# First feed-forward of a two-block model: gate borders as a ScalarE bias, gelu in PSUM, value taps moved, loops rotated

## The chip, the cores and the metric

One core of a Trainium2 chip runs the whole program. The metric is the device time of one execution in microseconds. In the text PE is TensorE (matmul), DVE is VectorE, ACT is ScalarE, POOL is GpSimd and SP is SyncE, which only issues loads here. SBUF is the working memory; PSUM is the memory that PE writes, eight banks of 128 x 512 f32.

## The reference

Two transformer-like blocks run one after the other on x of 1024 positions by 1024 channels, in f32. The change touches only the feed-forward of the first:

```python
h = _rmsnorm(x, ffn_pre_norm[l])
u = _causal_depthwise_conv(h @ w_up[l], conv_w[l], conv_b[l])    # CONV_WIDTH = 3
gate, val = jnp.split(u, 2, axis=-1)                             # D_FF = 2816 each
y = (jax.nn.gelu(gate, approximate=True) * val) @ w_down[l]
```

The convolution runs over the positions: each output is the bias plus three taps, of the same position and of the two before it. The feed-forward of the second block has no convolution.

## The kernel before

**Tiling.** Channels and features lie on the 128 partitions, positions along the free axis, in two halves LO and HI of HALF = 512. A "feature" n is a strip of 128 gate features and the 128 value features beside it; there are 22. Weights and activations are split into a high and a low part, and each product is three matmuls (high x high, high x low, low x high). Features 4 to 19 of each feed-forward are done in eight *pairs* with a fast scheme of seven block products where eight would be usual: one for the up product of each feature and one for the down product of the pair.

**PE.** `pair_up` (L1428) does seven `pair_block`s (L1415) of twelve matmuls for one feature; they go to bank 0 (gate, lower half), 1 (gate, upper half), 3 (value, upper half) and 2 (value, lower half), and DVE's sums complete them. `pair_down` (L1458) does seven blocks of four products into banks 4 to 7, each block into all four again. The order is: first feature of a pair, down product of the pair before, second feature. Each block waits for its bank to be read out (semaphores `lin_first`, `g_cv`, `p_prod`, `c_sum`, `p_lo`, `dn_free`) and for its weights (`unit_split`).

**DVE (L3338 to L3411).** `pair_unit1` is the work on one feature: `first_sums`, two gate taps of the lower half (`gate_taps`, L3348), `second_value` (completes bank 3), in a first feature `last_lows` of the pair before, `second_gate` (completes bank 1), a gate tap of the upper half, `first_value` (the last sum, completes bank 2), the other gate tap, and `edge_taps` (L3356): the two columns at the border of the halves need the last columns of bank 0, which ACT copied to EDGE because PE has filled bank 0 again by then. `gated_value` then does the value taps (L3367) and the product with gelu (L3373) for the upper half, and the same for the lower half, into banks 3 and 2. `first_blocks` and `second_blocks` form from these products the sums and the low parts for the down product (L3201, L3205). `pair_sums` (L3249) adds the 28 results of a down product to Y1t in SBUF. `pair_step1` strings these together and is the body of a loop.

**ACT (L2297 to L2405).** `gate_first` and `gate_second` write bias + third tap of the gate into ST_GATE in SBUF (L2302, L2309) and keep the border columns (L2304). `value_lin` (L2319) does the same for the value into ST_VALUE, `gelu_half` (L2314) works in place in ST_GATE. `product_high` and `sum_high` write high parts (L2188, L2192), `cast` writes high parts of weights (L2184). Its loop body is two times `pair_step1`: `first_up1`, `down_casts1`, `second_up1`. So it starts with `value_lin` and `gelu_half` of the second feature of the pair before.

**POOL** forms the weights' sums and low parts (L932, L939, L941, L944), and **SP** issues the weight loads.

Each engine runs its instructions in the order written out here; nothing is scheduled at run time. Behind the eighth pair comes a tail: two more features in halves (`half_tile` on PE, `unit_taps`, `product1` and `unit_low` on DVE), with the last pair's down product between them. In the tail DVE does the units' work first and then all of `pair_sums`.

## Time and profile before

| | us |
|---|---|
| median of 3 runs | 2838.39 (2836.68 to 2843.15) |
| the profiled execution | 2840.2, of which the span is 2838.4 |
| PE busy | 2702.7 (95%) |
| DVE busy | 1777.6 (63%) |
| POOL busy | 1700.1 (60%) |
| ACT busy | 971.9 (34%) |
| mean granted clock of PE | 0.987 |

The span is what the profile shows; the execution's time holds 1.8 us more around it. The features 4 to 19 of the first feed-forward lie at about 775 to 1333 us of the span, those of the second at about 2300 to 2778. In a timeline row the first two numbers are start and duration in us; "x28" says that a row merges 28 instructions; the bracket at the end is the time in which the engine did nothing before the row, and what ended it.

### The profile page before, as it was taken

Reading aid. Unit: us, or ns where it says so; the run is one execution under the profiler, and the core shown is the slowest. Engines: PE = TensorE matmul, PEld = TensorE weight load, DVE = VectorE, ACT = ScalarE, POOL = GpSimd, SP = SyncE. Lnnn points to the kernel's source line nnn. Section 1 sums busy time; section 2 is a strip of 40 time slices with the busy share of each in tenths; the row PEclk is TensorE's granted clock in tenths of the full one; section 3 lists DMA queues with packets and bytes.
Section 4 is the critical chain, followed back from the end, with each engine's and each line's share of the span. In section 5 each row is a group of like instructions: output and inputs, shape, how many; then the busy total and the mean of one; then the engine's idle time right before and its main releaser. Section 6 shows DMA issues by size and latency. Waiting matters only on the chain.

```text
span 2838.4 us, 39050 instructions
## 1 busy us (share of the span) xinstructions
PE 2702.7 (95%) x12922; PEld 2148.6 (76%) x12922; DVE 1777.6 (63%) x2540; ACT 971.9 (34%) x1941; POOL 1700.1 (60%) x1264
## 2 busy tenths in 40 slices
PE   8999999898989999998899999998999999999998
PEld 5777777686867777776678888777877878888887
DVE  6666687748568888877744311475536256766667
ACT  5544444435222233322423112555234222222222
POOL 4566311356988878875433334221355998888974
PEclk9999999999999999999999999999999999999999
DMA  4322221044111111114241234221444111111134
GB/s 143 101 89 88 92 90 49 12 147 161 38 52 53 53 49 52 52 50 157 90 144 49 59 107 141 88 73 53 141 148 165 51 49 56 57 55 55 53 123 141
DMA packets 89222, 243.01 MB, mean 86 GB/s; under 512 B 8527, under 2 KB 12400, under 8 KB 88692
## 3 DMA queue, kind: packets, MB, share of 16 engines
q1 hardware_dynamic: 66992, 183.27, 20.5%
q10 hardware_dynamic: 22084, 57.86, 5.8%
q8 instruction: 84, 1.38, 0.2%
q14 instruction: 62, 0.51, 0.1%
HBM read 205.95 MB, written 32.52 MB: 84 GB/s over the span
## 4 chain that ended last, share of the span: by engine, by line
PE 78%; DVE 11%; issue 4%; ACT 3%; POOL 3%; DMA 1%; DVEq 0%; POOLq 0%; ACTq 0%; SPq 0%
PE ps L1049 13%; PE ps L1051 12%; PE ps L1050 12%; PE ps L1422 6%; PE ps L1424 6%; PE ps L1423 6%; PE ps L1469 3%; PE ps L1471 3%; PE ps L1470 3%; PE ps L1140 2%; PE ps L1156 2%; PE ps L1704 1%; PE ps L1716 1%; PE ps L1171 1%; DVE ps L2954 1%
## 5 line engine op out<-in xcount | busy, mean ns | idle before, releaser
L797 POOL CAST wh<-raw 128x1024 fp32r<-128x1024 f32 x171 | 184.7, 1080 | 826.4 <-PE ps L1051 770.6
L1049 PE MATMUL ps<-hh,wh 128*128 128x512 f32 x1456 | 599.6, 412 | 24.9 <-DVE hl L2914 11.0
L1051 PE MATMUL ps<-hh,wl 128*128 128x512 f32 x1456 | 572.2, 393 | 0.0
L1050 PE MATMUL ps<-hl,wh 128*128 128x512 f32 x1456 | 570.7, 392 | 0.0
L799 POOL TENSOR_TENSOR wl<-raw,wh 128x1024 fp32r<-128x1024 f32 x171 | 412.5, 2412 | 13.7
L1049 PEld LDWEIGHTS ps<-hh,wh 128*128 128x128 f32 x1456 | 275.7, 189 | 97.6 <-issue 16.2
L1051 PEld LDWEIGHTS ps<-hh,wl 128*128 128x128 f32 x1456 | 274.8, 189 | 60.2
L1050 PEld LDWEIGHTS ps<-hl,wh 128*128 128x128 f32 x1456 | 275.8, 189 | 52.1 <-issue 3.4
L932 POOL TENSOR_TENSOR wl<-raw,wh 128x512 fp32r<-128x512 f32 x138 | 192.1, 1404 | 101.3 <-ACT wh L2184 100.8
L827 POOL TENSOR_TENSOR arena<-arena 128x1023 f32<-128x1023 f32 (+7 forms) x64 | 115.0, 1809 | 103.2 <-ACT arena L2041 100.8
L1423 PE MATMUL ps<-al,wh 128*128 128x512 f32 x420 | 165.6, 394 | 0.0
L3249 DVE TENSOR_TENSOR hlf<-ps,hlf 128x512 f32<-128x512 f32 x224 | 152.4, 691 | 20.9 <-PE ps L1471 19.0
L2184 ACT ACTIVATE wh<-raw 128x512 fp32r<-128x512 f32 x138 | 85.0, 627 | 203.6 <-PE ps L1471 134.2
L3249 DVE TENSOR_TENSOR arena<-ps,arena 128x512 f32<-128x512 f32 x224 | 146.8, 687 | 3.5 <-PE ps L1471 1.7
L3097 DVE TENSOR_TENSOR_SCAN arena<-arena,reset 128x1024 f32<-128x1024 f32 (+7 forms) x64 | 104.6, 1673 | 65.8 <-ACT arena L2038 65.8
L1049 PE MATMUL ps<-ah,wh 128*128 128x512 f32 x320 | 128.3, 401 | 5.8 <-DVE al L2986 3.1
L941 POOL TENSOR_TENSOR wl<-weight_sum,wh 128x512 fp32r<-128x512 f32 x92 | 124.4, 1353 | 7.4
L1051 PE MATMUL ps<-ah,wl 128*128 128x512 f32 x320 | 125.3, 392 | 0.0
L1050 PE MATMUL ps<-al,wh 128*128 128x512 f32 x320 | 125.1, 391 | 0.0
L2047 ACT ACTIVATE arena<-ps 128x512 f32<-128x512 f32 (+3 forms) x144 | 70.8, 492 | 158.6 <-PE ps L1156 158.0
L3183 DVE TENSOR_TENSOR ps<-ps,arena 128x512 f32<-128x512 f32 x96 | 66.9, 696 | 80.5 <-PE ps L1424 71.3
L1422 PE MATMUL ps<-hh,wh 128*128 128x512 f32 x240 | 96.4, 402 | 19.1 <-DVE block L3205 19.1
(412 smaller groups left out, 6334.3 us busy)
## 6 DMA issues: line engine op xcount, KB each, us to landing
raw<-weights SPq DMA_DIRECT2D x181, 512.0 KB, 3.6
raw<-weights SPq DMA_DIRECT2D x176, 256.0 KB, 2.6
arena<-w_ada SPq DMA_DIRECT2D x48, 512.0 KB, 3.8
arena<-gate_scratch ACTq DMA_DIRECT2D x20, 512.0 KB, 4.8
arena<-x_t ACTq DMA_DIRECT2D x1, 4096.0 KB, 14.0
x_scratch<-arena ACTq DMA_DIRECT2D x2, 2048.0 KB, 8.8
arena<-x_scratch SPq DMA_DIRECT2D x2, 2048.0 KB, 9.5
gate_scratch<-arena ACTq DMA_DIRECT2D x16, 256.0 KB, 2.4
```

Source lines behind the costliest of these rows:

```text
L797: pool.tensor_copy(wh[:, s], raw[:, r]).then_inc(Z.wt_hi, 1)
L799: pool.tensor_tensor(wl[:, s], raw[:, r], wh[:, s].bitcast(F32), ALU.subtract).then_inc(Z.split_done, 1)
L827: pool.tensor_tensor(beta[:, 0:w], beta[:, 0:w], S_U[u % 3][:, 1:w + 1], ALU.mult).then_inc(Z.s_a, 1)
L932: pool.tensor_tensor(wl[:, slot, w], src, wh[:, slot, w].bitcast(F32), ALU.subtract).then_inc(R.unit_split, 1)
L941: pool.tensor_tensor(wl[:, slot, w], src, wh[:, slot, w].bitcast(F32), ALU.subtract).then_inc(R.unit_split, 1)
L1049: pe.matmul(out, wh[:, slot, w], xh, start=start, stop=False)
L1050: pe.matmul(out, wh[:, slot, w], xl, start=False, stop=False)
L1051: return pe.matmul(out, wl[:, slot, w], xh, start=False, stop=stop)
L1422: pe.matmul(bank(b), wh[:, slot, t], xh, start=start and j == 0, stop=False, skip_group_check=True)
L1423: pe.matmul(bank(b), wh[:, slot, t], xl, start=False, stop=False, skip_group_check=True)
L1424: last = pe.matmul(bank(b), wl[:, slot, t], xh, start=False, stop=(j == 3), skip_group_check=True)
L3249: dve.tensor_tensor(t, bank(4 + f), t, ALU.add).then_inc(Z.dn_free, 1)
```

## The change

The change touches only the first feed-forward's pairs and the semaphore counts that go with them. It has five parts.

1. *Border columns on ACT.* `edge_taps` is gone from DVE. `gate_first` computes from the last two columns of bank 0 two bias columns (three one-column instructions and one wait for an own result), and `gate_second` adds its two border columns with these as bias (two one-column instructions) before the rest.
2. *Gelu of second features in PSUM.* `gelu_half` of a pair's second feature writes to bank 5 or 4, which are idle there, instead of ST_GATE; the product on DVE reads it there.
3. *Value taps ahead of the last sum.* In a second feature the upper half's value taps run before and behind `second_gate`, without the columns that need bank 2; those come after `first_value`, as two narrow taps (`value_edges`). ACT's `value_lin` for that half moves ahead of `gate_second`.
4. *Loops rotated.* ACT's loop body now starts with `down_casts1`, and DVE's with `pair_sums`. The order of the instructions is otherwise that of parts 1 to 3.
5. *Tail.* The first 12 of the last pair's 28 sums come ahead of the second unit's product and low part.

```diff
                         pe.wait_ge(R.lin_first, gate_lin(n, 0))
-                        pe.wait_ge(Z.g_cv, gate_taps_done(n, 2 - 6))
+                        pe.wait_ge(Z.g_cv, gate_taps_done(n, 2 - 4))
...
                 act.activation(ST_GATE[:, LO], bank(0), ACT.Identity, bias=conv_col(j, 3), scale=conv_col(j, 2)).then_inc(R.lin_first, 1)
                 pace(Z.g_cv, gate_taps_done(n, 0))
-                act.activation(EDGE, bank(0)[:, HALF - 2:], ACT.Copy).then_inc(R.lin_first, 1)
+                act.activation(EDGE[:, 0:1], bank(0)[:, HALF - 2:HALF - 1], ACT.Identity, bias=conv_col(j, 3), scale=conv_col(j, 0)).then_inc(R.lin_first, 1)
+                act.activation(EDGE[:, 1:2], bank(0)[:, HALF - 1:], ACT.Identity, bias=conv_col(j, 3), scale=conv_col(j, 0))
+                pace(R.lin_first, gate_lin(n, 2))
+                act.activation(EDGE[:, 0:1], bank(0)[:, HALF - 1:], ACT.Identity, bias=EDGE[:, 0:1], scale=conv_col(j, 1)).then_inc(R.lin_first, 1)
 
             def gate_second(n):
                 j = n + ST_FIRST
                 pace(R.c_sum, c_summed(0, n, 4))
-                act.activation(ST_GATE[:, HI], bank(1), ACT.Identity, bias=conv_col(j, 3), scale=conv_col(j, 2)).then_inc(Z.g_lin, 1)
-
-            def gelu_half(n, half):
-                pace(Z.g_cv, gate_taps_done(n, 6 if half else 2))
+                pace(R.lin_first, gate_lin(n, 3))
+                for r in range(2):
+                    act.activation(ST_GATE[:, HALF + r:HALF + r + 1], bank(1)[:, r:r + 1], ACT.Identity, bias=EDGE[:, r:r + 1], scale=conv_col(j, 2))
+                act.activation(ST_GATE[:, HALF + 2:], bank(1)[:, 2:], ACT.Identity, bias=conv_col(j, 3), scale=conv_col(j, 2)).then_inc(Z.g_lin, 1)
+
+            def gelu_half(n, half, second):
+                pace(Z.g_cv, gate_taps_done(n, 4 if half else 2))
                 t = ST_GATE[:, half_of(half)]
-                act.activation(t, t, ACT.Gelu_apprx_tanh).then_inc(Z.g_act, 1)
+                act.activation(bank(4 + half) if second else t, t, ACT.Gelu_apprx_tanh).then_inc(Z.g_act, 1)
...
                 value_lin(before, 0)
-                gelu_half(before, 1)
+                gelu_half(before, 1, True)
...
-                gelu_half(n, 0)
-                gate_second(n)
+                gelu_half(n, 0, True)
                 pace(R.p_prod, prods(0, n, 0))
                 value_lin(n, 1)
+                gate_second(n)
...
             pair_step1(1, 0, 2, 2)
+            first_up1(2, 1, 5, 5)
             with act.Fori(0, PAIR_LOOPS - 1) as i:
                 for u in range(2):
-                    pair_step1(i * 2 + (2 + u), i * 2 + (1 + u), i * 6 + (5 + 3 * u), 5 + 3 * u)
-            for u in range(2):
-                pair_step1(PAIRS - 2 + u, PAIRS - 3 + u, LAST_UP - 5 + 3 * u, 5 + 3 * u, u == 0)
+                    m, ks = i * 2 + (2 + u), 6 + 3 * u
+                    down_casts1(m, i * 6 + ks, ks)
+                    second_up1(m, i * 6 + (ks + 1), ks + 1)
+                    first_up1(i * 2 + (3 + u), m, i * 6 + (ks + 2), ks + 2)
+            down_casts1(PAIRS - 2, LAST_UP - 4, 6)
+            second_up1(PAIRS - 2, LAST_UP - 3, 7)
+            first_up1(PAIRS - 1, PAIRS - 2, LAST_UP - 2, 8)
+            down_casts1(PAIRS - 1, LAST_UP - 1, 9)
+            second_up1(PAIRS - 1, LAST_UP, 10, False)
             value_lin(ST_N - 1, 0)
...
-                    dve.wait_ge(R.lin_first, gate_lin(n, 2))
+                    dve.wait_ge(R.lin_first, gate_lin(n, 3))
...
-            def edge_taps(n):
-
-                j = n + ST_FIRST
+            def value_tap(pair, second, half, m, i, whole):
+
+                j = pair * 2 + (second + ST_FIRST)
+                if m:
+                    dve.wait_ge(Z.v_cv, value_taps_done(pair, second, i))
+                a, end = half * HALF + (0 if whole and half else 1 + m), (half + 1) * HALF
+                t = ST_VALUE[:, a:end]
+                dve.scalar_tensor_tensor(t, bank(2, 2)[:, a - 1 - m:end - 1 - m], conv_col(j, 5 - m), t, ALU.mult, ALU.add).then_inc(Z.v_cv, 1)
+
+            def value_edges(pair):
+
+                j = pair * 2 + (1 + ST_FIRST)
+                dve.wait_ge(Z.v_cv, value_taps_done(pair, 1, 2))
+                t = ST_VALUE[:, HALF:HALF + 2]
+                dve.scalar_tensor_tensor(t, bank(2)[:, HALF - 2:], conv_col(j, 4), t, ALU.mult, ALU.add).then_inc(Z.v_cv, 1)
+                dve.wait_ge(Z.v_cv, value_taps_done(pair, 1, 3))
+                t = ST_VALUE[:, HALF:HALF + 1]
+                dve.scalar_tensor_tensor(t, bank(2)[:, HALF - 1:], conv_col(j, 5), t, ALU.mult, ALU.add).then_inc(Z.v_cv, 1)
+
+            def gated_half(n, half, gelu):
+                dve.wait_ge(Z.g_act, n * 2 + (ST_FIRST + 1 + half))
+                dve.tensor_tensor(bank(2 + half), ST_VALUE[:, half_of(half)], gelu, ALU.mult).then_inc(R.p_prod, 1)
+
+            def first_gated(pair):
+
+                n = pair * 2
+                dve.wait_ge(Z.v_lin, n * 2 + (ST_FIRST + 2))
+                for half in (1, 0):
+                    for m in range(2):
+                        value_tap(pair, 0, half, m, 1 if half else 3, True)
+                    dve.wait_ge(Z.v_cv, value_taps_done(pair, 0, 2 if half else 4))
+                    gated_half(n, half, ST_GATE[:, half_of(half)])
+
+            def second_gated(pair):
+
+                n = pair * 2 + 1
+                dve.wait_ge(Z.v_lin, n * 2 + (ST_FIRST + 2))
+                value_edges(pair)
                 for m in range(2):
-                    dve.wait_ge(Z.g_cv, gate_taps_done(n, 4 + m))
-                    t = ST_GATE[:, HALF:HALF + 1 + m]
-                    dve.scalar_tensor_tensor(t, EDGE[:, 1 - m:], conv_col(j, 1 - m), t, ALU.mult, ALU.add).then_inc(Z.g_cv, 1)
-
-            def value_taps(n, half):
-
-                j, pair = n + ST_FIRST, bank(2, 2)
-                dve.wait_ge(Z.v_lin, n * 2 + (ST_FIRST + 2))
-                for m in range(2):
-                    if m:
-                        dve.wait_ge(Z.v_cv, value_taps_done(n, 1 if half else 3))
-                    a, end = max(half * HALF, 1 + m), (half + 1) * HALF
-                    t = ST_VALUE[:, a:end]
-                    dve.scalar_tensor_tensor(t, pair[:, a - 1 - m:end - 1 - m], conv_col(j, 5 - m), t, ALU.mult, ALU.add).then_inc(Z.v_cv, 1)
-
-            def gated_half(n, half):
-                t = half_of(half)
-                dve.wait_ge(Z.g_act, n * 2 + (ST_FIRST + 1 + half))
-                dve.wait_ge(Z.v_cv, value_taps_done(n, 2 if half else 4))
-                dve.tensor_tensor(bank(2 + half), ST_VALUE[:, t], ST_GATE[:, t], ALU.mult).then_inc(R.p_prod, 1)
-
-            def gated_value(n):
-                for half in (1, 0):
-                    value_taps(n, half)
-                    gated_half(n, half)
-
-            def pair_unit1(n, k, lows_left):
-
+                    value_tap(pair, 1, 0, m, 5, False)
+                gated_half(n, 1, bank(5))
+                dve.wait_ge(Z.v_cv, value_taps_done(pair, 1, 6))
+                gated_half(n, 0, bank(4))
+
+            def first_unit1(pair, k, lows_left):
+
+                n = pair * 2
                 first_sums(0, n, k)
                 gate_taps(n, 0, 0)
                 gate_taps(n, 0, 1)
                 gate_taps(n, 1, 0)
                 first_value(0, n, k)
                 gate_taps(n, 1, 1)
-                edge_taps(n)
-
-            def pair_step1(m, prev, k):
-
-                gated_value(prev * 2 + 1)
+
+            def second_unit1(pair, k):
+
+                n = pair * 2 + 1
+                first_sums(0, n, k)
+                gate_taps(n, 0, 0)
+                gate_taps(n, 0, 1)
+                second_value(0, n, k)
+                dve.wait_ge(Z.v_lin, n * 2 + (ST_FIRST + 1))
+                value_tap(pair, 1, 1, 0, 0, False)
+                second_gate(0, n, k)
+                value_tap(pair, 1, 1, 1, 1, False)
+                gate_taps(n, 1, 0)
+                first_value(0, n, k)
+                gate_taps(n, 1, 1)
+
+            def pair_end1(prev, m, k):
+
+                second_gated(prev)
                 second_blocks(0, prev)
-                pair_unit1(m * 2, k, prev)
-                pair_sums(0, Y1t, prev, k + 1)
-                gated_value(m * 2)
+                first_unit1(m, k, prev)
+
+            def pair_begin1(m, prev, k):
+
+                pair_sums(0, Y1t, prev, k)
+                first_gated(m)
                 first_blocks(0, m)
-                pair_unit1(m * 2 + 1, k + 2, None)
-
-            pair_unit1(0, 0, None)
+                second_unit1(m, k + 1)
+
+            first_unit1(0, 0, None)
             down_sums(Y1t, ST_FIRST - 1, 0, None, unit_done(0, 7))
-            gated_value(0)
+            first_gated(0)
             first_blocks(0, 0)
-            pair_unit1(1, 1, None)
-            pair_step1(1, 0, 2)
+            second_unit1(0, 1)
+            pair_end1(0, 1, 2)
             with dve.Fori(0, PAIRS - 2) as i:
-                pair_step1(i + 2, i + 1, i * 3 + 5)
-            gated_value(ST_N - 1)
+                pair_begin1(i + 1, i, i * 3 + 3)
+                pair_end1(i + 1, i + 2, i * 3 + 5)
+            pair_begin1(PAIRS - 1, PAIRS - 2, LAST_UP - 1)
+            second_gated(PAIRS - 1)
             second_blocks(0, PAIRS - 1)
             last_lows(0, PAIRS - 1)
             dve.sem_inc(Z.f_prod, ST_N)
             for u in range(2):
                 unit_taps(1, u, 0)
                 unit_taps(1, u, 1)
+                if u:
+                    pair_sums(0, Y1t, PAIRS - 1, LAST_DOWN, 0, 3)
                 product1(1, u)
                 unit_low(1, u)
-            pair_sums(0, Y1t, PAIRS - 1, LAST_DOWN)
+            pair_sums(0, Y1t, PAIRS - 1, LAST_DOWN, 3)
             dve.wait_ge(Z.dn_free, 4 + DN_FFN)
             dve.wait_ge(Z.fold, 4)
             for f in range(KT):
```

## Rows read from the trace of the kernel before

**Rows 1.** profile page, part 1: busy time, share of the span, instructions.

```profile
PE 2702.7 (95%) x12922; PEld 2148.6 (76%) x12922; DVE 1777.6 (63%) x2540; ACT 971.9 (34%) x1941; POOL 1700.1 (60%) x1264
```

**Rows 2.** waits of PE, first feed-forward's pairs: us, times, longest.

```profile
PE ps L1422 <- DVE block L3205: 19.1, 7, 3.7
PE ps L1469 <- DVE arena L3249: 11.2, 8, 4.5
```

**Rows 3.** stretches: length; busy PE, PEld, DVE, ACT, POOL; clock, DMA share, GB/s.

```profile
846.20:1280.10 433.90, 410.37 (x1752) 332.02 (x1752) 362.11 (x504) 130.69 (x223) 354.19 (x305) 0.98 0.17 53
2346.80:2743.90 397.10, 397.10 (x1742) 326.40 (x1741) 268.78 (x369) 88.91 (x155) 346.44 (x305) 1.00 0.19 60
```

**Rows 4.** timeline of PE: start us, us, instruction [idle before, releaser].

```profile
1049.00 0.50 PE L1469 MATMUL ps<-gated,wh 128*128 128x512 f32 x1 [0.93 <-DVE arena L3249]
...
1092.85 0.39 PE L1424 MATMUL ps<-hh,wl 128*128 128x512 f32 x1
1095.88 0.49 PE L1422 MATMUL ps<-hh,wh 128*128 128x512 f32 x1 [2.64 <-DVE block L3205]
...
1098.76 0.63 PE L1422 MATMUL ps<-hh,wh 128*128 128x512 f32 x1
```

**Rows 5.** timeline of DVE, end of one second feature's unit.

```profile
1082.40 0.70 DVE L3183 TENSOR_TENSOR ps<-ps,arena 128x512 f32<-128x512 f32 x1 [1.87 <-PE ps L1424]
...
1085.21 0.70 DVE L3183 TENSOR_TENSOR ps<-ps,arena 128x512 f32<-128x512 f32 x1 [0.40 <-PE ps L1424]
...
1086.59 1.60 DVE L3356 SCALAR_TENSOR_TENSOR arena<-dsm,cols,arena 128x1 f32<-128x1 f32 x2
1088.32 1.65 DVE L3367 SCALAR_TENSOR_TENSOR arena<-ps,cols,arena 128x512 f32<-128x512 f32 x2
1090.00 0.70 DVE L3373 TENSOR_TENSOR ps<-arena 128x512 f32<-128x512 f32 x1
...
1092.17 1.78 DVE L3373 TENSOR_TENSOR ps<-arena 128x512 f32<-128x512 f32 x1
...
1095.07 0.67 DVE L3205 TENSOR_TENSOR block<-ps,block 128x512 fp32r<-128x512 f32 x1
```

**Rows 6.** timeline of ACT in the same unit.

```profile
1083.24 0.78 ACT L2309 ACTIVATE arena<-ps,cols 128x512 f32<-128x512 f32 x1 [2.57 <-DVE ps L3183]
...
1086.04 0.78 ACT L2319 ACTIVATE arena<-ps,cols 128x512 f32<-128x512 f32 x1 [1.35 <-DVE ps L3183]
```

**Rows 7.** lines L3373, L2224, L3296: duration in ns, least/median/most.

```profile
L3373 DVE TENSOR_TENSOR ps<-arena x32: 699/1060/1793, 818.9 to 1283.6; 128x512 f32<-128x512 f32 x32
...
L2224 ACT ACTIVATE arena<-ps,dsm,cols x16: 334/343/352, 681.2 to 1368.9; 128x1 f32<-128x1 f32 x16
...
L3296 DVE SCALAR_TENSOR_TENSOR dsm<-ps,cols,dsm x8: 204/207/211, 680.9 to 1308.8; 128x1 f32<-128x1 f32 x8
```

**Rows 8.** timeline of ACT where its loop starts again.

```profile
1024.77 0.78 ACT L2319 ACTIVATE arena<-ps,cols 128x512 f32<-128x512 f32 x1 [3.08 <-issue]
```

**Rows 9.** timeline of DVE, start of one pair's down sums.

```profile
1048.27 18.46 DVE L3249 TENSOR_TENSOR arena<-ps,arena 128x512 f32<-128x512 f32 x28
```

**Rows 10.** timeline of DVE, then PE and ACT, at the first pair.

```profile
803.44 2.39 DVE L3356 SCALAR_TENSOR_TENSOR arena<-dsm,cols,arena 128x1 f32<-128x1 f32 x2
...
806.57 0.47 PE L1049 MATMUL ps<-gated,wh 128*128 128x512 f32 x1 [2.41 <-DVE arena L3263]
...
799.55 0.63 ACT L2184 ACTIVATE wh<-raw 128x512 fp32r<-128x512 f32 x1 [15.40 <-DMA raw<-weights]
```

**Rows 11.** timeline of DVE, then PE, behind the last pair.

```profile
1276.30 2.97 DVE L3356 SCALAR_TENSOR_TENSOR arena<-dsm,cols,arena 128x1 f32<-128x1 f32 x2
...
1312.62 3.24 DVE L3249 TENSOR_TENSOR arena<-ps,arena 128x512 f32<-128x512 f32 x5
...
1287.81 0.80 PE L1049 MATMUL ps<-hh,wh 128*128 128x512 f32 x1 [7.58 <-DVE gated L3205]
...
1313.44 0.77 PE L1469 MATMUL ps<-gated,wh 128*128 128x512 f32 x1 [4.46 <-DVE arena L3249]
```

More of the change, by code:

```diff
@@ L649, in gate_taps_done, with value_taps_done @@
         def gate_taps_done(n, i):
-            return n * 6 + (2 * ST_FIRST + i)
-        def value_taps_done(n, i):
             return n * 4 + (2 * ST_FIRST + i)
+        def value_taps_done(pair, second, i):
+            return pair * 10 + (2 * ST_FIRST + 4 * second + i)
         def gate_lin(n, i):
-            return n * 2 + (2 * (A_N - SB_N) + i)
+            return n * 3 + (2 * (A_N - SB_N) + i)
         def wt_slot(c):
@@ L2385, in _ @@
             cast(0, 1, 1, False, 0)
-            gelu_half(0, 0)
+            gelu_half(0, 0, False)
             gate_second(0)
             cast(0, 1, 1, False, 1)
-            gelu_half(0, 1)
+            gelu_half(0, 1, False)
             value_lin(0, 1)
@@ L3233, in last_lows, with pair_sums @@
                 block_low(use, pair, 8, S4_L, S4_F, S4_H)
-            def pair_sums(use, y, pair, k):
+            def pair_sums(use, y, pair, k, first=0, end=ST_BLOCKS):
                 free = DN_FFN * use + 16 * ST_FIRST
-                dve.wait_ge(Z.dn_free, pair * PAIR_SUMS + (free + 4))
-                for u in range(ST_BLOCKS):
+                if first == 0:
+                    dve.wait_ge(Z.dn_free, pair * PAIR_SUMS + (free + 4))
+                for u in range(first, end):
                     f0, half = D_OUT[u]
```

12 lines of the change are left out of this document (6 added, 6 removed).

## The prediction

> **What bounds the kernel now.** I read the page's first part, then where TensorE (PE) waits, then the same stretch of work in the two feed-forwards, then single waits in the timeline. The page says that PE is the bound: 2702.7 us busy, 95% of the span [rows 1]. A change to the other engines can only give back time in which PE waits, or runs at its lower clock. The list of PE's waits in the first feed-forward's pair stage has two repeated entries: seven before L1422 (19.1 us) and eight before L1469 (11.2 us) [rows 2].
>
> How much is that worth in full? The second feed-forward does the same pair work with other code on DVE and ACT. I cut the same 1752 matmuls out of both: from the wait before the second pair to the last matmul before the tail's first wait. They take 433.9 us in the first and 397.1 us in the second, where PE never waits and the granted clock is 1.00 instead of 0.98 [rows 3]. So 36.8 us can be had here, and no more. POOL, whose work is the same in both, is busy 346 us in the 397 us stretch, so it is no floor above it.
>
> Two waits make up the difference in each pair.
> - The *block wait*: in a pair's first feature, block 3 (bank 3) may start once DVE has written the low half of block22 of the pair before (L3205). PE idles 2.64 us at 1095.88 [rows 4] and up to 3.7; seven in all [rows 2].
> - The *sum wait*: in a pair's down product, the second block needs bank 4 back, that is, the first sum of L3249. PE idles 0.93 us at 1049.00 [rows 4], because DVE comes to its sums only at 1048.27 [rows 9].
>
> Behind four of the seven block waits some nine matmuls run at half the clock: at 1098.76 a matmul shows 0.63 us where the one at 1092.85 shows 0.39 [rows 4]; that is 0.2 us for each, about 1.8 a stretch, 7 in all. In the second feed-forward's stretch, without waits, the clock never falls [rows 3].
>
> **The block wait, step by step.** I follow the unit that ends before 1095.88. PE's last matmul before the wait started at 1092.85 [rows 4]; at the pitch of 397.1 / 1752 = 0.227 us [rows 3] the next would have started at 1093.08. So the low half has to be there 2.8 us earlier. The chain on DVE [rows 5]: last sum (first_value) 1085.21 to 1085.90, second gate tap, edge taps 1086.59 to 1088.19, value taps of the upper half from 1088.32 (1.65), product 0.70, value taps of the lower half 1.5, product 1092.17 (1.78), two sums, low half 1095.07 to 1095.74.
>
> What the change takes out of it:
> - The two edge taps: 1.60 us, and 0.13 to the next. They go to ACT (below).
> - The upper half's value taps, 1.65 us: they move ahead of the last sum. Only two narrow ones stay behind (value_edges). Narrow taps with one PSUM source are L3296: 207 ns each [rows 7], 0.4 in all.
> - The slow products. L3373 takes 699 ns at best, 1060 in the median, 1793 at most [rows 7]; here 0.70 and 1.78 [rows 5]. Both inputs lie in SBUF. In the same stretch 0.67 us is what L3205 takes with one input in PSUM [rows 5]. With gelu's output in banks 4 and 5 both products of a second feature have a PSUM input: I take 0.70 each, 1.08 us less here.
>
> New times: gate tap ends 1086.55; ACT's last value_lin ends 1086.82 [rows 6] and stays a condition; value_edges to 1087.3; two taps (0.75 each) to 1088.8; product to 1089.5; second product to 1090.1. ACT's copy of block22's high half follows the first product (about 0.75 us), so the two sums and the low half (0.6 each) run from 1090.25 to 1092.1. PE resumes by 1092.3 and wanted 1093.08. The block wait goes, with 0.8 us to spare. What is late next is nothing of DVE's: block 4 needs another low half 1.2 us later, and PE comes to it 2.7 us later.
>
> What is put ahead: the upper value taps sit before and behind second_gate in the second feature's unit. DVE idled 1.87 us before it and 0.40 us before the last sum [rows 5], 1.0 more for ACT's gate_second between them; two taps are 1.5 us. The first waits for ACT's value_lin, now ahead of gate_second: ACT idled 2.57 us there [rows 6]. So all of it fits, and costs nothing while that idle time is there; if it is not, up to 1.5 us a pair returns, of which 0.8 is covered.
>
> What ACT gets: in gate_second two narrow ops with a column as bias come first. Those are L2224, 343 ns each [rows 7], issued at a pitch of about a quarter us: 0.5 us before the wide one. In gate_first the bias columns take three such ops and a wait on itself, about 0.9 us instead of 0.16; its product is needed over 2 us later, so that is free. ACT is busy 131 of 434 us [rows 3].
>
> **The sum wait.** At 1048.27 DVE starts its 28 sums, straight behind the edge taps (1.5 us). Without these and with gate_second 0.5 us later, they start 1.0 us earlier. PE idled 0.93 us. About 0.1 us stays, perhaps 0.2 with a loop's restart: 7 x 0.2 = 1.4 us.
>
> **The rotated loops.** ACT's loop restarted in front of the value_lin that the block wait hangs on. There it idled 3.08 us put down to "issue" [rows 8] against 1.35 in the unit of [rows 6]: 1.73 us more, and the block wait behind it is the longest, 3.7 [rows 2]. Now it restarts where ACT waits for PE anyway. DVE's loop restarted behind the edge taps, where 0.13 us shows; now it restarts in front of the sums, where nothing covers it. Its cost there is not shown: between 0.13 (the same loop at its old place) and 1.73 (ACT's). I take 0.13, since it is the same engine. By ACT's price six restarts would give back 10.4 us. The Trainium skill ("Advanced Engine Details and Errata", Control Flow Timing) gives 108 ns for a compare-and-branch, which would make it 0.6 us in all; ACT's row at the restart does not agree with it, DVE's does.
>
> **Before and behind.** At the first pair the edge taps took 2.39 us (803.44) just before the sums that PE waited 2.41 us for (806.57) [rows 10]: 2.39 - 0.5 = 1.9 us, and 0.6 of the 2 us at half clock behind it: 2.5. Bounds 1.5 and 4.4.
>
> Behind the last pair PE waits 7.58 us at 1287.81 for the same chain, two steps further; its edge taps took 2.97 us (1276.30) [rows 11]. Worked as above: 2.97 + 1.5 (taps) + 1.0 (products) - 0.4 - 0.4 (waits for ACT) = 4.7 us, and 0.5 of clock: 5.2. Bounds 4.0 and 7.0.
>
> In the last down product PE waits 4.46 us (1313.44) for sums that start at 1312.62 [rows 11]. Twelve sums now come before the last product and its low half, so they start 3.5 us earlier; but the 28 sums are then cut by product and low half (some 3.5 us with ACT's copy between), and PE comes to the fourth block's bank in that time: it waits about 1.1 and then 3.2. So the wait is mostly moved. I take 1.2 us, for fewer matmuls at half clock; bounds -1 and 4.5.
>
> **Sum.** 36.8 - 1.4 - 0.4 (a little clock) = 35.0; 2.5; 5.2; 1.2: 43.9 us. The profiled execution took 2840.2 us (span 2838.4 and 1.8 around it), the median of three is 2838.39. 2840.2 - 43.9 = 2796.3, and by the median 2794.5: I say 2796.
>
> **Rivals.**
> - *The chain is cut by less* (23%). DVE's restart costs ACT's 1.73 us in front of the sums (10.4); the taps put ahead, or products still held, leave 0.4 us of block wait in seven pairs (2.8); and with waits left some stretches at half clock stay (about 5 of the 7 us). 43.9 - 18.2 = 25.7: 2814. For it: the spare time is only 0.8 us of a chain of ten steps. Against: DVE's restart shows 0.13 us now.
> - *ACT holds DVE in the second unit* (3%, slower). Until now only the gate waited behind ACT's weight cast in that unit; with the change DVE stops at a value tap before second_gate, so everything behind it waits as well. ACT has stood 15.40 us for a weight load ahead of such a cast (799.55) [rows 10]. Its queue is idle 2.2 us before the gelu there and 0.8 is spare, so up to 3 us of lateness costs nothing; slower than before it becomes from about 3 + 6.3 (43.9 / 7) = 9 us of lateness in each pair. At 15.4 each pair loses 12.4: 7 x 12.4 - 43.9 = +43, so 2883. Against: DMA is busy 17% of the stage, and 19% in the second feed-forward's faster one [rows 3].
> - *It doesn't do what it says* (3%): the chain ends elsewhere, for example on POOL's casts, and the time stays within 5 us: 2838.
>
> **How the numbers follow.** Forecast 71%, its own range 2788 to 2806 (all bounds of the terms: 36.8 + 4.4 + 7 + 4.5 = 52.7 at best, 35 + 1.5 + 4 - 1 - 5 = 34.5 at worst). To hold 8 in 10 the range reaches into the first rival: 2788 to 2814. A difference of 0.2% is about what a measurement of this kernel can tell from none. Faster by more: 71 + 23 + 1 = 95%; within: 2%; slower: 3%.
>
> **What would show it.** In the changed kernel's profile: L1422 and the first L1469 of a down product wait for DVE nowhere, or under 0.3 us; the stretch of 1752 matmuls takes 397 to 401 us at clock 1.00; the second features' products take about 0.70 us, the first features' still 0.7 to 1.8; the wait behind the last pair is about 3 us; in the last down product one wait of 1 us and one of 3. It would be wrong if a block wait over 0.5 us is left in most pairs, if DVE idles over 0.5 us in front of its 28 sums, or if the products with gelu in PSUM still take over 1 us.

## The result, and the profile after

The changed kernel takes 2794.05 us (median of four runs, 2792.95 to 2795.16) where the kernel before takes 2838.74 in the same comparison: ratio 0.9841, 95% interval 0.9823 to 0.9858. The forecast was 2796. The profiled execution of after took 2794.4 us (span 2792.6) against 2840.2: 45.8 us less, where the sum said 43.9.

First part of the page of after (busy us, share of the span, instructions), which answers to [rows 1]:

```profile
PE 2692.7 (96%) x12922; PEld 2144.4 (77%) x12922; DVE 1737.9 (62%) x2524; ACT 990.8 (35%) x2005; POOL 1694.8 (61%) x1264
```

PE's busy time fell by 10.0 us for the same number of matmuls: that is work that ran at half the clock before. The rest, 36 us, was idle time. PE's waits in the first feed-forward's pairs and behind them (us, times, longest), which answer to [rows 2, 11]:

```profile
PE ps L1049 <- DVE gated L3218: 2.8, 1, 2.8
...
PE ps L1469 <- DVE arena L3263: 1.5, 2, 0.8
PE ps L1049 <- DVE arena L3277: 0.8, 1, 0.8
```

There is no line for L1422 any more: the seven block waits are gone. L3263 is the down sum that was L3249, and its two waits lie in the last down product; of the seven sum waits of the pairs nothing is left that the list shows. L3218 is the line of the wait behind the last pair: 2.8 us, where it was 7.58.

The first stretch of [rows 3] in after, and the same 1752 matmuls of the second feed-forward in after and in before (length; busy PE, PEld, DVE, ACT, POOL; clock, DMA share, GB/s):

```profile
839.00:1240.20 401.20, 401.19 (x1753) 328.31 (x1751) 334.07 (x494) 148.33 (x280) 350.10 (x306) 1.00 0.18 57
2295.41:2695.33 399.92, 399.92 (x1754) 328.84 (x1752) 270.96 (x372) 89.28 (x156) 349.28 (x306) 1.00 0.18 57
```

```profile
2341.43:2741.35 399.92, 399.92 (x1754) 328.76 (x1752) 271.33 (x372) 89.43 (x156) 349.61 (x306) 1.00 0.19 57
```

(A row also counts matmuls that it only touches.) The first feed-forward's stretch is now PE's own work at clock 1.00, 1.3 us above the second's. The second row of [rows 3], 397.10 us, is not this cut: it starts 5.4 us later and holds 2.8 us of matmuls less, as its count of 1742 beside 1752 says. DVE lost 28 us against [rows 3], ACT gained 18, POOL lost 4.

To see where the time went I cut each profiled execution at the same matmuls. A: first block product of the first pair (L1371) to the first L1422. B: from there to the start of the last down product, with the wait behind the last pair. C: the last down product. L1277 comes behind it in pairs. D: the end of C to the third such pair. E: the fourth pair to L1774 (the 20.5 us between the third and the fourth are the same in all kernels and left out). F: L1774 to the first L1371 of the second feed-forward. (us, worked out from the start times of these matmuls)

```
          A      B       C      D      E       F
before  41.69  489.63  26.73  70.10  477.19  377.57
after   38.44  449.17  21.40  72.04  478.40  378.68
gain     3.25   40.46   5.33  -1.94   -1.21   -1.11
```

The stage that the change touches gained 49.0 us, and 4.3 of them were lost again in D, E and F, code that it does not touch; another 0.3 us went behind F. Before A after led by 1.4 us, which is no work of the change.

### The profile page after: what moved, and what is told of

It reads as the page before. It is cut to its first block, busy times and chain, and to the rows that moved or that the text cites. A ratio compares the mean times of both kernels' runs of the same rounds, so it can differ in the third digit from the quotient of the medians.

```text
span 2792.6 us, 39158 instructions
## 1 busy us (share of the span) xinstructions
PE 2692.7 (96%) x12922; PEld 2144.4 (77%) x12922; DVE 1737.9 (62%) x2524; ACT 990.8 (35%) x2005; POOL 1694.8 (61%) x1264
## 4 chain that ended last, share of the span: by engine, by line
PE 81%; DVE 9%; ACT 3%; POOL 3%; issue 2%; DMA 1%; POOLq 0%; DVEq 0%; ACTq 0%; SPq 0%
PE ps L1049 13%; PE ps L1051 13%; PE ps L1050 13%; PE ps L1422 7%; PE ps L1424 7%; PE ps L1423 7%; PE ps L1469 4%; PE ps L1471 4%; PE ps L1470 4%; PE ps L1140 2%; PE ps L1156 2%; PE ps L1704 1%; PE ps L1716 1%; PE ps L1171 1%; DVE ps L2967 1%
## 5 line engine op out<-in xcount | busy, mean ns | idle before, releaser
L1049 PE MATMUL ps<-hh,wh 128*128 128x512 f32 x1456 | 600.9, 413 | 20.0 <-DVE hl L2927 10.8
L799 POOL TENSOR_TENSOR wl<-raw,wh 128x1024 fp32r<-128x1024 f32 x171 | 412.3, 2411 | 13.7
L932 POOL TENSOR_TENSOR wl<-raw,wh 128x512 fp32r<-128x512 f32 x138 | 190.1, 1392 | 71.9 <-ACT wh L2184 71.2
L3263 DVE TENSOR_TENSOR hlf<-ps,hlf 128x512 f32<-128x512 f32 x224 | 152.4, 691 | 20.9 <-PE ps L1471 19.0
L3263 DVE TENSOR_TENSOR arena<-ps,arena 128x512 f32<-128x512 f32 x224 | 145.5, 686 | 1.6
L1469 PE MATMUL ps<-sums,wh 128*128 128x512 f32 x256 | 101.3, 396 | 0.0
```

The source lines that it names most:

```text
L799: pool.tensor_tensor(wl[:, s], raw[:, r], wh[:, s].bitcast(F32), ALU.subtract).then_inc(Z.split_done, 1)
L932: pool.tensor_tensor(wl[:, slot, w], src, wh[:, slot, w].bitcast(F32), ALU.subtract).then_inc(R.unit_split, 1)
L1049: pe.matmul(out, wh[:, slot, w], xh, start=start, stop=False)
L1469: pe.matmul(bank(4 + f), wh[:, slot, t], xh, start=u in D_FRESH, stop=False, skip_group_check=True)
L3263: dve.tensor_tensor(t, bank(4 + f), t, ALU.add).then_inc(Z.dn_free, 1)
```

## The experiments

Each is timed against the kernel before on the same chip; its edit is told against after, but for the kernel that puts part 1 alone on before. The diffs show the main lines of each edit; the semaphore counts and arguments that follow from them are left out. None leaves out a part of the computation.

**Part 1 undone**: the border columns are DVE's edge taps again, the rest stays.

```diff
-                act.activation(EDGE[:, 0:1], bank(0)[:, HALF - 2:HALF - 1], ...)
...
+                act.activation(EDGE, bank(0)[:, HALF - 2:], ACT.Copy).then_inc(R.lin_first, 1)
...
                 gate_taps(n, 1, 1)
+                edge_taps(n)
```

> The changed kernel with its part 1 undone: the border columns are DVE's edge taps again, ACT copies two columns and writes all of the upper half at once; gelu in PSUM, value taps ahead, rotated loops and the tail stay. Theory (a chain with 0.83 us to spare in front of block 3): the edge taps put 1.7 us back into the chain, of which 0.8 is covered: a block wait of 0.9 us in seven pairs (6.3), the sum wait of 0.9 us in seven pairs (6), 1.9 at the first pair, 2 to 3 behind the last: 2794 + 17 = 2811, more if stretches at half clock come back (up to 7). Rival (no spare time, every us of the chain counts): 1.7 x 7 + 6 + 4.5 = 23: 2817. Rival (the edges are hidden as well): under 2797.

Measured: 2814.33 us, ratio 0.9906 (0.9888 to 0.9925): 20 us of the gain are gone. Its waits of PE, its DVE at the end of a second feature's unit, and two waits in its PE timeline:

```profile
PE ps L1469 <- DVE arena L3257: 7.8, 8, 1.1
...
PE ps L1422 <- POOL wl L932: 0.6, 4, 0.2
```

```profile
1071.54 1.61 DVE L3364 SCALAR_TENSOR_TENSOR arena<-dsm,cols,arena 128x1 f32<-128x1 f32 x2
1073.08 0.21 DVE L3380 SCALAR_TENSOR_TENSOR arena<-ps,cols,arena 128x2 f32<-128x2 f32 x1
...
1077.54 0.68 DVE L3212 TENSOR_TENSOR block<-ps,block 128x512 fp32r<-128x512 f32 x1
```

```profile
1078.35 0.49 PE L1422 MATMUL ps<-hh,wh 128*128 128x512 f32 x1 [0.16 <-POOL wl L932]
1093.24 0.50 PE L1469 MATMUL ps<-gated,wh 128*128 128x512 f32 x1 [1.00 <-DVE arena L3257]
```

The sum wait is back in full (1.0 us a pair); the block wait stays small, though the edge taps again take 1.61 us in front of it. They cost the chain less than their length: ACT's last value_lin, for which DVE otherwise idles 0.39 us, now ends beside them, and without the narrow ops gate_second is 0.5 us shorter. The wait is named after POOL; DVE's low half, which ends at 1078.22, came last (the added operations below show it). So part 1 is the cure of the sum wait, and parts 2 to 4 nearly cure the block wait without it. By the segments 3.1 us of the 20 lie in A, 13.6 in B and 3.7 in F, where the two programs are the same. The 3.7 us in F come from one narrow DVE instruction with both inputs in SBUF, which ends with POOL's row:

```profile
1899.88 2.37 POOL L799 TENSOR_TENSOR wl<-raw,wh 128x1024 fp32r<-128x1024 f32 x1
1900.06 2.21 DVE L3692 TENSOR_TENSOR wsm<-cols,wsm 128x4 f32<-128x4 f32 x1
...
1902.30 0.47 ACT L2648 ACTIVATE arena<-ps,wsm 128x256 f32<-128x256 f32 x1 [1.94 <-DVE wsm L3692]
```

```profile
1903.95 1.09 PE L1761 MATMUL ps<-mats,arena 128*128 128x128 f32 x4 [2.10 <-ACT arena L2657]
```

At the same place of after's code this instruction takes 0.16 us. ACT and then PE wait for it, and the matmuls behind PE's wait run at half the clock (0.63 us at 1905.27 for 0.40 at 1901.22). So this part of the 20 us is no work of the edge taps: it depends on what POOL does at that moment. The two kernels reach the place 16 us apart; that this is what lets the two meet is not shown.

**Part 1 alone on the kernel before.**

```diff
-                act.activation(EDGE, bank(0)[:, HALF - 2:], ACT.Copy).then_inc(R.lin_first, 1)
+                act.activation(EDGE[:, 0:1], bank(0)[:, HALF - 2:HALF - 1], ACT.Identity, bias=conv_col(j, 3), scale=conv_col(j, 0)).then_inc(R.lin_first, 1)
...
                 gate_taps(n, 1, 1)
-                edge_taps(n)
```

> The kernel before with part 1 alone: the border columns on ACT; gelu in SBUF, value taps behind the last sum, loops and tail as before. Theory (chain arithmetic): the value taps can start 1.3 us earlier (they then wait for ACT's value_lin instead of the edge taps), so of the block wait's 2.8 us 1.5 are left in six pairs and about 2.5 where ACT's loop restarts; the sum wait goes; behind the last pair 5 us of wait are left, and 4.5 in the last down product. 2794.5 + 7 x 1.6 + 1 + 3 = 2810, up to 2817 with stretches at half clock. Rival (the parts only work together): over 2825. Rival (part 1 is all that matters): 2797 or less.

Measured: 2811.16 us, ratio 0.9892 (0.9874 to 0.991). Its waits:

```profile
PE ps L1422 <- DVE block L3213: 8.0, 7, 1.2
...
PE ps L1049 <- DVE gated L3213: 4.8, 1, 4.8
...
PE ps L1469 <- DVE arena L3258: 4.5, 1, 4.5
```

Part 1 alone brings 1.08% of 1.59%: the seven sum waits, and the block waits from 19.1 us to 8.0. For the last 8.0 us part 3 is enough beside part 1: no block wait is left without parts 2 and 4 (below), and 2.2 us without part 3. The 4.5 us in the last down product are untouched, as in before.

**Parts 2, 3 and 4, each undone.** Part 2: gelu of second features back in ST_GATE.

```diff
-                act.activation(bank(4 + half) if second else t, t, ACT.Gelu_apprx_tanh).then_inc(Z.g_act, 1)
+                act.activation(t, t, ACT.Gelu_apprx_tanh).then_inc(Z.g_act, 1)
...
-                gated_half(n, 1, bank(5))
+                gated_half(n, 1, ST_GATE[:, HI])
```

> The changed kernel with part 2 undone: gelu of second features goes back into SBUF. Theory: the two products of a second feature take longer by what POOL holds them, in the mean 2 x 0.36 = 0.7 us a pair (median 1060 against 699 ns), which the spare 0.83 us covers in most pairs: under 0.3 us of block wait, and about 1 us behind the last pair: 2795 to 2797. Rival (no spare): 0.7 to 1.1 us in seven pairs and the tail: 2800 to 2803. Rival (the products are not slower than now): 2794, and the two products under 0.75 us each.

Part 3: all value taps behind the last sum.

```diff
                 second_value(0, n, k)
-                dve.wait_ge(Z.v_lin, n * 2 + (ST_FIRST + 1))
-                value_tap(pair, 1, 1, 0, 0, False)
                 second_gate(0, n, k)
-                value_tap(pair, 1, 1, 1, 1, False)
```

> The changed kernel with part 3 undone: in second features both halves' value taps come behind the last sum again, and ACT's value_lin behind gate_second; the rest stays. Theory: the chain grows by 1.65 - 0.44 = 1.2 us, less 0.83 spare: block waits of 0.4 us in seven pairs (with the restart 0.5 each) and 1.2 behind the last pair: 2794 + 4.7 = 2799. Rival (no spare): 1.2 x 8 = 10: 2804. Rival (the taps put ahead delayed second_gate and cost what they saved): 2794 or less.

Part 4: both loops start where they did before.

```diff
             pair_end1(0, 1, 2)
+            pair_begin1(1, 0, 3)
             with dve.Fori(0, PAIRS - 2) as i:
-                pair_begin1(i + 1, i, i * 3 + 3)
                 pair_end1(i + 1, i + 2, i * 3 + 5)
-            pair_begin1(PAIRS - 1, PAIRS - 2, LAST_UP - 1)
+                pair_begin1(i + 2, i + 1, i * 3 + 6)
```

> The changed kernel with part 4 undone: ACT's loop starts with first_up1 and DVE's with second_gated again, the order of the instructions is that of the changed kernel. Theory: ACT's restart (1.7 us, once) falls on the chain and is covered but for 0.9 us; DVE's restarts leave the place in front of the sums, where they show 0.1 us or less: 2794 to 2796. Rival (the rotation is what made the waits go): 2804 or more, with block waits in all pairs that a restart precedes.

Measured: 2795.02 (ratio 0.9837, 0.9819 to 0.9854), 2798.12 (0.985, 0.9833 to 0.9867) and 2795.37 (0.9837, 0.982 to 0.9854). Without part 2 no block wait comes back, only 0.7 us behind the last pair (3.5 for 2.8): all products read SBUF alone again and take 1100 ns in the median, and the spare time covers them. Its B is 2.1 us longer than after's and its D 2.2 us shorter (table below), so that the time of the whole hides what B shows. Without part 3 six block waits are left, of up to 0.4 us, and B is 5.5 us longer, of which D gives back 2.1; its ratio of 0.985 is one that after itself gets below, so the times alone do not show a loss, the waits do:

```profile
PE ps L1049 <- DVE gated L3218: 3.8, 1, 3.8
...
PE ps L1422 <- DVE block L3218: 2.2, 6, 0.4
```

Without part 4 there is neither a block wait nor a difference in time. ACT's loop starts again at 1009.64 there, in front of a value_lin, and nothing starts again at the one of the pair before, 951.63:

```profile
951.63 0.78 ACT L2325 ACTIVATE arena<-ps,cols 128x512 f32<-128x512 f32 x1 [1.53 <-DVE ps L3191]
```

```profile
1009.64 0.78 ACT L2325 ACTIVATE arena<-ps,cols 128x512 f32<-128x512 f32 x1 [1.71 <-DVE ps L3191]
```

The restart costs 0.18 us, and as much with part 1 alone (1.03 for 0.85), where ACT's loop also starts as in before. The 3.08 us of [rows 8] come back in neither.

**Parts 2 and 4 undone together**, for if each is covered by the same spare time, two might not be; the edit is the two above.

> The changed kernel with parts 2 and 4 undone together, since each alone was worth nothing measurable (2795.0 and 2795.4). Theory (each is covered by the chain's spare 0.9 us, together they may use it up): 0.7 us of held products in each pair, 1.7 once more at ACT's restart: 1.5 us of block wait once and none or 0.2 elsewhere, 0.7 more behind the last pair: 2796 to 2798. Rival (the spare is used up in every pair): 2801 or more.

Measured: 2793.57 us (0.9842, 0.9827 to 0.9857), and no block wait. Both parts can go and nothing is lost that the times can show; in its profile B is 2.4 us longer than after's and D 2.1 us shorter. It is not a better version either.

**How much is spare.** To all pairs but the last I add DVE operations of 1024 columns, which write to a buffer that nobody reads, behind the wait for the last value_lin. One:

```diff
                 dve.wait_ge(Z.v_lin, n * 2 + (ST_FIRST + 2))
+                if not isinstance(pair, int) or pair < PAIRS - 1:
+                    dve.tensor_tensor(T(21)[:, 0:1024], bank(6, 2)[:, 0:1024], hh_read[:, 0], ALU.add)
                 value_edges(pair)
```

> The changed kernel with one instruction of 1024 columns more on DVE, ahead of value_edges in all pairs but the last (it sums PSUM and SBUF into a dead buffer, about 1.25 us). Theory: 0.83 us are spare, so a block wait of about 0.4 us appears in seven pairs: 2794 + 7 x 0.5 = 2797.5. Rival (no spare): 1.25 x 7 = 9: 2803. Rival (more is spare): no block wait, 2794. Stretches at half clock: none or few at a wait this short.

Two: the same, and once more between the last two value taps.

> As the one before with two such instructions (about 2.5 us), the second between the lower half's value taps. Theory: a block wait of 1.7 us in seven pairs, 11.9 + 0.7, and up to 1.8 us of half clock behind each: 2807 without, up to 2819 with it. The rise from the kernel with one such instruction is 1.25 us a pair, all of it, since the spare time is used up. It tells whether waits of 1.7 us bring the stretches at half clock back; the waits of 2.5 to 3.7 us of the kernel before brought four in seven.

Measured: 2794.45 (0.9846, 0.9829 to 0.9862) and 2801.39 (0.9873, 0.9856 to 0.9889). The operations that the second kernel adds, and then its PE:

```profile
1067.48 1.23 DVE L3402 TENSOR_TENSOR arena<-ps,hh 128x1024 f32<-128x1024 f32 x1 [0.30 <-ACT arena L2325]
...
1069.66 1.21 DVE L3406 TENSOR_TENSOR arena<-ps,hh 128x1024 f32<-128x1024 f32 x1
...
1074.09 0.68 DVE L3218 TENSOR_TENSOR block<-ps,block 128x512 fp32r<-128x512 f32 x1
```

```profile
1074.90 0.49 PE L1422 MATMUL ps<-hh,wh 128*128 128x512 f32 x1 [1.16 <-POOL wl L932]
```

The row names POOL, but what came last is DVE's low half, which ends at 1074.77. The same row of the kernel with one operation shows 0.17 us of idle time. A row's idle time counts from the end of a matmul of 0.39 us, at a pitch of 0.227, so the block is 0.16 us later than the idle time says: 0.33 us late with one operation, which pushes the chain by 1.14 (1067.48 to 1068.62), and 1.32 with two. So 1.14 - 0.33 = 0.8 or 2.28 - 1.32 = 1.0 us is spare. Both kernels are faster than expected. With one operation the block waits are there, but B is only 2.0 us longer and D 2.2 us shorter. With two, the waits are 1.2 us where 1.7 was expected. The waits for L1422 in the second kernel's list:

```profile
PE ps L1422 <- POOL wl L932: 6.8, 6, 1.2
...
PE ps L1422 <- DVE block L3218: 1.0, 1, 1.0
```

Its B is 456.44 us, 7.3 longer than after's, no more than these waits: behind the seven of them no matmul runs at half the clock (granted 1.00 from 810.69 to 1242.00).

**Part 5 undone**: the last pair's 28 sums in one piece, behind the last product.

```diff
-                if u:
-                    pair_sums(0, Y1t, PAIRS - 1, LAST_DOWN, 0, 3)
                 product1(1, u)
                 unit_low(1, u)
-            pair_sums(0, Y1t, PAIRS - 1, LAST_DOWN, 3)
+            pair_sums(0, Y1t, PAIRS - 1, LAST_DOWN)
```

> The changed kernel with part 5 undone: all 28 sums of the last pair come behind the second tail unit's product and low part. My prediction's step (the wait is mostly moved) expected 1.2 us of part 5 and would have this kernel at 2795. What the first profile of the change shows (4.46 us before, 0.78 and 0.71 after, and no stretch at half clock) makes it 3 us of wait and 1 to 2.7 of clock: 2797 to 2800, with one wait of about 4.5 us at the second block of the last down product.

Measured: 2794.86 us (0.9846, 0.983 to 0.9862), no slower than after, and a miss. The wait is back, and behind it the half clock (PE of this kernel):

```profile
1269.91 0.77 PE L1469 MATMUL ps<-gated,wh 128*128 128x512 f32 x1 [4.46 <-DVE arena L3263]
...
1273.88 0.63 PE L1469 MATMUL ps<-gated,wh 128*128 128x512 f32 x1
...
1275.16 0.47 PE L1469 MATMUL ps<-sums,wh 128*128 128x512 f32 x1
```

By the segments C is 26.62, 5.2 us longer than after's, and D, E and F together are 4.4 us shorter. This made two theories: the gain of part 5 is real and given back later, or the single comparison missed it. So after was measured again, in three rounds beside it,

> The changed kernel once more, for the 4.7 us that its first profile lost against the one of before behind the last pair's stage (lead 50.5 us at the end of the last down product, 45.8 at the end). If that is drift from run to run (other stretches at half clock), the lead at the end differs by a microsecond or two from the first profile and the losses sit elsewhere. If something behind the tail takes the gain back, the same 4.7 us are lost at the same places. Time 2793 to 2796.

with 2795.28 us (0.985, 0.9834 to 0.9867), and then both in five rounds beside each other:

> The changed kernel in five rounds, beside the same without part 5, to settle what part 5 is worth in the whole. Both have been within 1 us of each other so far (2794.05 and 2795.28 against 2794.86), although the last down product takes 21.4 us with part 5 and 26.6 without it. Theory (what part 5 saves is lost again at half clock behind it: 0 to 2.3 us before the second mean, 1.2 and 1.2 in the second block's attention): 2794 to 2795.5, about 1 us under the other. Rival (the profiles mislead and all 5.2 us count): 5 us under the other.

> The changed kernel without part 5, once more and in five rounds. Theory: 0 to 2 us above the changed kernel of the same job (2795 to 2796.5); the last down product takes 26.6 us instead of 21.4, the rest behind it 4 us less. Rival: 5 us above.

Measured: after 2794.36 us (0.984, 0.9827 to 0.9854), without part 5 2794.91 (0.9848, 0.9835 to 0.9862). The segments, in us:

```
                    B       C      D      E       F
after             449.17  21.40  72.04  478.40  378.68
again, 3 rounds   449.43  21.40  72.19  478.37  378.74
again, 5 rounds   449.37  21.38  72.30  478.35  378.79
no 5, 3 rounds    449.39  26.62  70.00  477.16  377.56
no 5, 5 rounds    449.43  26.79  70.10  477.20  377.53
no 3              454.63  21.40  69.91  478.32  378.95
no 2              451.22  21.40  69.84  478.33  378.94
part 1 alone      461.44  25.70  72.48  478.41  378.97
no 1              462.79  21.38  72.30  478.35  382.36
no 4              449.37  21.36  72.23  478.38  378.78
no 2, no 4        451.61  21.40  69.96  478.40  379.01
one added         451.17  21.38  69.88  478.34  378.97
two added         456.44  21.38  72.19  478.40  378.76
```

Beside each other, part 5 saves 5.2 us in C (three rounds) and 5.4 (five), and D, E and F give 4.6 of it back each time: 0.6 and 0.8 are left. The medians show -0.4 in three rounds and 0.5 in five, which is no difference. It is given back at the granted clock, not in waits. D, and the end of E, where nearly all of E's difference lies, in after (columns as above),

```profile
1282.37:1354.41 72.04, 62.35 (x248) 48.36 (x247) 54.99 (x83) 32.95 (x56) 35.59 (x22) 0.93 0.33 107
1816.40:1853.30 36.90, 31.75 (x166) 23.85 (x165) 31.78 (x74) 19.29 (x83) 10.22 (x6) 0.91 0.24 79
```

and without part 5:

```profile
1289.19:1359.19 70.00, 60.29 (x248) 46.57 (x247) 54.96 (x83) 32.97 (x56) 35.57 (x22) 0.95 0.33 108
1821.20:1856.90 35.70, 30.56 (x168) 23.23 (x167) 31.79 (x74) 19.22 (x83) 10.20 (x6) 0.95 0.26 81
```

DVE and ACT do the same in both, 55.0 and 33.0 us in D and 31.8 and 19.2 in the second row of each; PE has the same matmuls and the lower clock, 0.93 for 0.95 and 0.91 for 0.95. Why it falls there is open. In all profiles D takes one of two lengths, 69.8 to 70.1 us or 72.0 to 72.5, and E 477.2 or 478.4. Part 5 is not the only condition: with part 1 alone, where the 28 sums are in one piece, D, E and F are as long as in after; and without part 2 or part 3, or with one added operation, D is short while E and F are long. So two kernels can differ by 2 us in D alone, with no difference in D's code.

## Why the prediction was right, and where it wasn't

By the lead of after over before, read off along PE's matmuls:

*Pair stage: predicted 35.0, measured 35.3.* This carried the forecast. The mechanism held: both waits went, for the reason given. That the size agrees to 0.3 us is partly luck, since the bound of 36.8 us [rows 3] has two errors that stand against each other. The second feed-forward's row is not cut at the same 1752 matmuls: these take 399.9 us, so that the stretch held 34.0 us and not 36.8. And the stretch of 433.9 us begins behind the first of the seven block waits, not before it, so that this wait is in no term:

```profile
846.19 0.50 PE L1422 MATMUL ps<-hh,wh 128*128 128x512 f32 x1 [2.37 <-DVE block L3205]
```

From matmul to matmul it is 2.5 us. Together 36.5 us could be had. After took 35.3: 32.7 in the stretch (433.9 to 401.2) and 2.5 in front of it. The 401.2 us lie 0.2 above the 397 to 401 given, and the lower end of that range could not be reached: PE's own work there takes 399.9.

*The block wait's new chain: predicted 5.55 us from the end of the gate tap to the end of the low half, measured 5.56.* After's DVE in the unit that answers to [rows 5]:

```profile
1062.56 0.74 DVE L3362 SCALAR_TENSOR_TENSOR arena<-ps,cols,arena 128x510 f32<-128x510 f32 x1
1063.70 0.22 DVE L3378 SCALAR_TENSOR_TENSOR arena<-ps,cols,arena 128x2 f32<-128x2 f32 x1 [0.39 <-ACT arena L2325]
1063.95 0.22 DVE L3381 SCALAR_TENSOR_TENSOR arena<-ps,cols,arena 128x1 f32<-128x1 f32 x1
1064.09 1.53 DVE L3371 SCALAR_TENSOR_TENSOR arena<-ps,cols,arena 128x511 f32<-128x511 f32 x2
1065.53 1.29 DVE L3385 TENSOR_TENSOR ps<-arena,ps 128x512 f32<-128x512 f32 x2
1066.97 0.69 DVE L3214 TENSOR_TENSOR sums_f<-ps,arena 128x512 f32<-128x512 f32 x1 [0.15 <-ACT block L2188]
...
1068.18 0.68 DVE L3218 TENSOR_TENSOR block<-ps,block 128x512 fp32r<-128x512 f32 x1
```

The low half ends at 1068.86; PE takes block 3 at 1069.69 without a wait:

```profile
1069.69 0.39 PE L1422 MATMUL ps<-hh,wh 128*128 128x512 f32 x1
```

0.8 us to spare was predicted, 0.83 is in these rows, and about 0.9 in the two kernels with added operations.

*Products with gelu in PSUM: predicted 0.70 each; they take 684 to 692 ns,* the first features' (both inputs in SBUF) 700 to 1161. In before the same line ranged up to 1793 [rows 7]. The same holds of the narrow taps: 220 ns with a PSUM source (L3378, all eight within 4 ns), where the edge taps with all inputs in SBUF took 219 to 2449 in before. The Trainium skill ("SBUF — State Buffer", Who interferes with whom) says that a DVE instruction with two SBUF inputs contends with a GpSimd instruction that reads SBUF, and that one with at most one SBUF input, outside the 2-port modes, does not. The trace agrees in every row of these lines. But the gain hung less on this than the prediction said: without part 2 the products take 1100 ns again and no block wait comes back.

*ACT's narrow ops: predicted 0.5 us ahead of the wide one; 0.49* (1060.00 to 1060.49):

```profile
1060.00 0.59 ACT L2314 ACTIVATE arena<-ps,dsm,cols 128x1 f32<-128x1 f32 x2 [1.77 <-DVE ps L3196]
1060.49 0.78 ACT L2315 ACTIVATE arena<-ps,cols 128x510 f32<-128x510 f32 x1
```

*The sum wait: predicted 0.2 us a pair,* with a restart of DVE's loop in it at the price of 0.13. Four of the seven pairs show some 0.16 us, three none. PE's row of one, where the matmul ahead of it starts at 1083.07 and the pitch is 0.227:

```profile
1083.07 0.39 PE L1471 MATMUL ps<-gated,wl 128*128 128x512 f32 x1
1083.46 0.50 PE L1469 MATMUL ps<-gated,wh 128*128 128x512 f32 x1
```

No gap stands in front of DVE's sums at the restart, and the kernel with the old loop starts is no slower. So the restart costs at most the 0.13 us taken, and the rival's 1.73 was wrong, for ACT too: its restart shows 0.18 us in the two kernels whose loop starts as in before. The Trainium skill's 108 ns for a compare-and-branch ("Advanced Engine Details and Errata", Control Flow Timing) speaks for the same side. What made the 3.08 us of [rows 8], in one profile, stays open; the restart by itself did not.

*First pair: predicted 2.5, measured 3.3.* The wait fell from 2.41 us [rows 10] to 0.78, less than the 1.9 said; the clock gave more than the 0.6 said. This term is not steady: in the two further profiles of after the wait is 0.3 and 1.9 us, and A gains 3.7 and 2.2.

*Behind the last pair: predicted 5.2, measured 5.2*, with a wait of 2.8 us left where "about 3" was said.

*Last down product: predicted 1.2, measured 5.3. This term was mis-sized.* The prediction said "the wait is mostly moved", 1.1 and then 3.2 us. DVE of after there, and PE's two waits:

```profile
1263.81 7.38 DVE L3263 TENSOR_TENSOR arena<-ps,arena 128x512 f32<-128x512 f32 x12
1271.11 0.68 DVE L3317 TENSOR_TENSOR arena<-arena 128x512 f32<-128x512 f32 x1
1272.49 0.69 DVE L3018 TENSOR_TENSOR gated<-arena,gated 128x512 fp32r<-128x512 f32 x1 [0.70 <-ACT gated L1941]
1273.10 10.17 DVE L3263 TENSOR_TENSOR arena<-ps,arena 128x512 f32<-128x512 f32 x16
```

```profile
1264.63 0.47 PE L1469 MATMUL ps<-gated,wh 128*128 128x512 f32 x1 [0.78 <-DVE arena L3263]
...
1273.92 0.47 PE L1469 MATMUL ps<-block,wh 128*128 128x512 f32 x1 [0.71 <-DVE arena L3263]
```

The sums are cut for 2.0 us (1271.11 to 1273.10), not 3.5: I had priced product and low half as held by POOL, and here they were not (0.68 and 0.69; the first unit's, at 1253.12, took 1.73). (Without part 5 the same two take 1.21 and 1.67, so how POOL holds them depends on the moment.) So the second wait is 0.71 and not 3.2. The waits fell by 3.0 us, and the half clock behind them (2.3 us) went too.

*Missing from the sum: 4.6 us lost behind the last down product*, at the granted clock. Nothing in the working looked beyond the changed stage. It made up for the mis-sized term: 3.3, 35.3, 5.2 and 5.3 are 49.0 before rounding, and with the 1.4 by which the execution led before the stage, less 4.6, 45.8. The total was good to 2 us in part because two errors of over 4 us stood against each other.

Of the rivals, "the chain is cut by less" put 2.8 us of left block waits, 10.4 of restarts and 5 of half clock: none showed in the pairs. "ACT holds DVE": DVE's wait in front of the tap that was put ahead is 1.18 us at most in the unit shown (1058.37), where DVE stood idle before as well [rows 5].

## What to carry to other kernels

Find all waits that one chain makes and ask what is spare once the first few steps are cut: here 28.7 of some 45 us came from the cheapest part, and two of the other four only add to 0.9 us that is spare anyway. Undone one by one the five parts are worth 20 (3.7 of them by the narrow instruction in F), 1, 4, 1 and 1 us, and by the times only the first is surely more than nothing. So the sum over parts undone is not the gain: parts that shorten one chain stand in for each other, and one kernel with a part alone is needed to see it. A stretch of the same work in another part of the same kernel, without waits, is a better bound than any sum of waits, since it holds the clock too, but both have to be cut at the same instructions: counts of 1752 and 1742 beside each other hid 2.8 us here.

## What the runs showed of the hardware

- Waits of 1.0 to 1.2 us on PE, seven in one stage, brought no half clock (granted 1.00 over the 431 us that hold them). Of the seven waits of 2.4 to 3.7 us in before, the four of 2.6 to 2.7 us at 969.57, 1095.88, 1159.23 and 1222.30 brought it, 1.4 to 1.7 us each, and the longest, 3.7 us at 1034.17, did not. A wait of 4.5 us brought 2.3 to 2.4 us in three kernels and 1.3 with part 1 alone. So the length of a wait alone does not decide it.
- The granted clock of a stretch can differ by what went before: DVE, ACT and the matmuls the same, 36.90 and 35.70 us at 0.91 and 0.95. Over 500 us behind the last changed instruction this still takes back 1.2 us of a gain. Three profiles of after show it alike, and so do both of the kernel without part 5, so it is not chance; what sets it stays open.
- A wait that the profile puts down to POOL (1.16 us, L932) was DVE's: it grew from 0.17 to 1.16 with one more DVE operation, and POOL's work was not touched.
- One DVE instruction of 128x4 with both inputs in SBUF took 2.21 us beside POOL's L799 where after's took 0.16 at the same place, and through ACT and the clock cost PE 3.7 us (part 1 undone, 1900.06).
